# Depthwise convolution in a fused encoder kernel: 28 taps of two channel tiles go to GpSimd, 14 taps of the last tile go from TensorE to VectorE

## The reference, cut to what matters

```python
u = proj[..., Q_DIM + 2 * KV_DIM:]                    # 1024 columns
u = u[..., :CONV_CH] * jax.nn.sigmoid(u[..., CONV_CH:])     # gated: 512 channels
u = conv_general_dilated(u, conv_w[:, None, :], padding 15 on both sides,
                         feature_group_count=CONV_CH) + conv_b   # 31 taps, each channel by itself
c_out = silu(layer_norm(u, cln_g, cln_b))             # mean and variance over the 512 channels
mix = concatenate([a_out, c_out]); out = mix @ w_out
```

## Time and profile before

| | |
|---|---|
| median of 3 executions | 1344.31 us (1344.28 to 1344.64) |
| span of the profiled execution, first to last instruction | 1342.5 us |
| what lies around the span, against the median | 1.8 us |
| TensorE busy | 1335.2 us, 99% |
| VectorE busy | 1157.7 us, 86% |
| ScalarE busy | 1007.8 us, 75% |
| GpSimd busy | 44.5 us, 3% |
| the stage of the change | 16 to 104 us of the span |

### The profile page before, as it was taken

How to read it: one execution, slowest core, us unless ns; L and a number is a source line. 1 busy time by engine, 2 the same in 40 slices (tenths; PEclk the granted TensorE clock), 3 DMA queues, 4 the chain that set the end, 5 groups by cost and what they waited for, 6 DMA issues and landing times.

```text
span 1342.5 us, 19094 instructions
## 1 busy us (share of the span) xinstructions
PE 1335.2 (99%) x6779; PEld 1130.5 (84%) x6779; DVE 1157.7 (86%) x1257; ACT 1007.8 (75%) x1189; POOL 44.5 (3%) x55
## 2 busy tenths in 40 slices
PE   9999999999999999999999999999999999999998
PEld 8879999988888888888888888888888888888887
DVE  7986655557899999999999999999999999999996
ACT  7776444447878887888878788888888787888885
POOL 2000000000003000000000000000000000000100
PEclk9999999999999999999999999999999999999999
DMA  9409843476899899999999989999999999999930
GB/s 347 172 1 340 294 167 126 135 283 184 183 388 398 308 396 395 343 390 396 395 338 396 394 339 392 396 395 338 396 394 364 368 396 395 394 394 397 398 151 34
DMA packets 178661, 426.51 MB, mean 318 GB/s; under 512 B 4145, under 2 KB 14001, under 8 KB 178609
## 3 DMA queue, kind: packets, MB, share of 16 engines
q1 hardware_dynamic: 173712, 412.56, 82.1%
q0 software_dynamic: 3024, 11.01, 3.3%
q10 hardware_dynamic: 1872, 2.26, 0.5%
HBM read 419.53 MB, written 6.29 MB: 317 GB/s over the span
## 4 chain that ended last, share of the span: by engine, by line
PE 97%; DVE 2%; ACT 1%; DMA 0%; issue 0%; POOL 0%; ACTq 0%; DVEq 0%; POOLq 0%
PE G L1483 19%; PE G L1485 19%; PE G L1484 19%; PE Y L1483 11%; PE Y L1485 11%; PE Y L1484 11%; PE G L1887 2%; PE G L1677 1%; PE G L1715 1%; DVE ring L966 1%; PE Y L1685 0%; PE Y L1508 0%; DMA h<-in_x 0%; PE G L1806 0%; PE Y L1705 0%; DVE lo_ring L886 0%
## 5 line engine op out<-in xcount | busy, mean ns | idle before, releaser
L886 DVE TENSOR_TENSOR lo_ring<-ring,hi_ring 128x1024 fp32r<-128x1024 f32 x691 | 836.2, 1223 | 132.0 <-ACT hi_ring L517 92.4
L517 ACT ACTIVATE hi_ring<-ring 128x1024 fp32r<-128x1024 f32 x691 | 731.5, 1061 | 244.4 <-PE G L1485 149.8
L1483 PE MATMUL G<-hi_ring,xT_hi 128*128 128x512 f32 x896 | 353.6, 395 | 0.0
L1485 PE MATMUL G<-lo_ring,xT_hi 128*128 128x512 f32 x896 | 349.5, 390 | 0.0
L1484 PE MATMUL G<-hi_ring,xT_lo 128*128 128x512 f32 x896 | 348.8, 389 | 0.0
L1483 PE MATMUL Y<-hi_ring,mT_hi 128*128 128x512 f32 x568 | 224.1, 395 | 0.0
L1485 PE MATMUL Y<-lo_ring,mT_hi 128*128 128x512 f32 x568 | 221.4, 390 | 0.0
L1484 PE MATMUL Y<-hi_ring,mT_lo 128*128 128x512 f32 x568 | 221.2, 389 | 0.0
L1485 PEld LDWEIGHTS G<-lo_ring,xT_hi 128*128 128x128 f32 x896 | 168.2, 188 | 35.9
L1484 PEld LDWEIGHTS G<-hi_ring,xT_lo 128*128 128x128 f32 x896 | 168.3, 188 | 33.6
L1483 PEld LDWEIGHTS G<-hi_ring,xT_hi 128*128 128x128 f32 x896 | 168.3, 188 | 33.5 <-DVE lo_ring L886 0.3
(11 more groups left out here) (262 smaller groups left out, 947.8 us busy)
## 6 DMA issues: line engine op xcount, KB each, us to landing
ring<-in_moe_wg SPq DMA_DIRECT2D x56, 2048.0 KB, 12.2
ring<-in_moe_wu SPq DMA_DIRECT2D x56, 2048.0 KB, 13.2
ring<-in_moe_wd SPq DMA_DIRECT2D x56, 2048.0 KB, 13.1
ring<-in_ffn_wg SPq DMA_DIRECT2D x5, 2048.0 KB, 14.3
ring<-in_ffn_wu SPq DMA_DIRECT2D x5, 2048.0 KB, 12.9
ring<-in_ffn_wd SPq DMA_DIRECT2D x5, 2048.0 KB, 9.1
ring<-in_ple_gate_w SPq DMA_DIRECT2D x4, 2048.0 KB, 7.8
ring<-in_w_in SPq DMA_DIRECT2D x4, 1024.0 KB, 14.9
```

What stands on the lines that cost most here:

```text
L517: act.activation(hi_ring[:, n % AHEAD, :], where, ACT.Copy).then_inc(hi_done, 1)
L886: dve.tensor_tensor(lo_ring[:, n % AHEAD, :], where, hi_ring[:, n % AHEAD, :].bitcast(F32), ALU.subtract).then_inc(lo_done, 1)
L1483: pe.matmul(dst, s_hi, m_hi, start=start, stop=False, skip_group_check=True)
L1485: return pe.matmul(dst, s_hi, m_lo, start=False, stop=stop, skip_group_check=True)
```

## The change

The last 14 taps (17 to 30) of tiles 0 and 1 leave VectorE's queue. GpSimd makes them for both tiles at once, in 128x512 operations: a product into `side`, then 13 times a product into `side_part` and an addition to `side`, each waiting for the one before. VectorE adds `side` to tiles 0 and 1 behind its loop. Taps 0 to 13 of tile 3 leave TensorE (and their diagonals leave ScalarE) and become VectorE taps beside those of tile 2. TensorE keeps 17 taps of tile 3, and VectorE adds their sum from PSUM, in place of ScalarE's copy. `LATE_TAPS` has 45 entries instead of 59.

```diff
-PE_TAPS = tuple((3, k) for k in range(CONV_W))
+VECTOR_TAPS = 14
+PE_TAPS = tuple((3, k) for k in range(VECTOR_TAPS, CONV_W))
 EARLY_TAPS = tuple((c, k) for k in range(1, EARLY_ROWS) for c in range(2))
-LATE_TAPS = late_taps()
+LATE_TAPS = tuple((c, k) for k in range(CONV_W) for c in (2, 3) if c == 2 or k < VECTOR_TAPS)
+CONV_STEPS = (EARLY_ROWS + 1, EARLY_ROWS + 1, CONV_W, VECTOR_TAPS + 1)
-STEP_TAPS = (6, 6, 2, 3, 3, 2, 3, 3, 3, 0)
-assert sum(STEP_TAPS) == CONV_W
+STEP_TAPS = (4, 3, 1, 2, 1, 1, 2, 1, 2, 0)
+assert sum(STEP_TAPS) == len(PE_TAPS)
...
+    side = carve(2 * SEQ).rearrange("p (c n) -> p c n", c=2)
+    side_part = carve(2 * SEQ).rearrange("p (c n) -> p c n", c=2)
...
     (ScalarE, behind its loop)
-        act.wait_ge(conv_mm, 1)
-        act.activation(conv[:, 3, :], G[:, 3, 0:SEQ], ACT.Identity, bias=conv_b[:, 3:4]).then_inc(conv_out, 1)
...
     (VectorE, behind its loop)
+        dve.wait_ge(conv_mm, 1)
+        dve.wait_ge(conv_v[3], VECTOR_TAPS)
+        dve.tensor_tensor(conv[:, 3, :], conv[:, 3, :], G[:, 3, 0:SEQ], ALU.add).then_inc(conv_v[3], 1)
+        dve.wait_ge(side_step, 2 * (CONV_W - EARLY_ROWS) - 1)
+        for c in range(2):
+            dve.tensor_tensor(conv[:, c, :], conv[:, c, :], side[:, c, :], ALU.add).then_inc(conv_v[c], 1)
         taps(late, len(late))
         o_low(CT - 1)
         lo_upto(11 + AHEAD)
...
     (GpSimd, behind the rotary table)
+        pool.wait_ge(vec_in, 16)
+        pool.wait_ge(glu_done, 1)
+        for n, k in enumerate(range(EARLY_ROWS, CONV_W)):
+            weight = conv_w[:, 0:2, k:k + 1].broadcast_to([P, 2, SEQ])
+            if n == 0:
+                pool.tensor_tensor(side[:, :, :], upad[:, 0:2, k:k + SEQ], weight, ALU.mult).then_inc(side_step, 1)
+                continue
+            pool.wait_ge(side_step, 2 * n - 1)
+            pool.tensor_tensor(side_part[:, :, :], upad[:, 0:2, k:k + SEQ], weight, ALU.mult).then_inc(side_step, 1)
+            pool.wait_ge(side_step, 2 * n)
+            pool.tensor_tensor(side[:, :, :], side[:, :, :], side_part[:, :, :], ALU.add).then_inc(side_step, 1)
```

More of the change, by code:

```diff
@@ L345, in kernel_program @@
     qk_tr, qk_tr_copied = sem("qk_tr"), sem("qk_tr_copied")
[L346 to L349, removed]
+    sig_done, glu_done, zeros_set = sem("sig_done"), sem("glu_done"), sem("zeros_set")
+    conv_v = [sem(f"conv_v{c}") for c in range(CT)]
+    side_step = sem("side_step")
+    diag_a, conv_mm = sem("diag_a"), sem("conv_mm")
+    table_set, q_sq, k_sq = sem("table_set"), sem("q_sq"), sem("k_sq")
     sc_done, neg_done, exp_done, nrm_done = sem("sc_done"), sem("neg_done"), sem("exp_done"), sem("nrm_done")
@@ L615, in _ @@
         act.activation(qT[:, :, :], Y[:, 0:2, :].rearrange("p b (k n) -> p (b k) n", k=2), ACT.Copy).then_inc(qk_tr_copied, 1)
-        act.wait_ge(k_zero, 1)
+        act.wait_ge(zeros_set, 2)
         for u in range(2):
@@ L974, in taps @@
             del todo[:n]
-        dve.wait_ge(pads_set, 1)
+        dve.wait_ge(zeros_set, 1)
         glu(0)
@@ L1051, in _ @@
         lo_upto(11 + AHEAD)
-        for c in range(3):
-            dve.wait_ge(conv_v[c], CONV_W)
+        for c in range(CT):
+            dve.wait_ge(conv_v[c], CONV_STEPS[c])
         dve.wait_ge(mean_mm, 1)
@@ L1372, in _ @@
         pool.memset(upad[:, :, 0:PAD], 0.0)
-        pool.memset(upad[:, :, PAD + SEQ:], 0.0).then_inc(pads_set, 1)
-        pool.memset(kT[:, :, :, :], 0.0).then_inc(k_zero, 1)
+        pool.memset(upad[:, :, PAD + SEQ:], 0.0).then_inc(zeros_set, 1)
+        pool.memset(kT[:, :, :, :], 0.0).then_inc(zeros_set, 1)
         pool.wait_ge(cst_in, 16)
@@ L1723, in _ @@
         pe.wait_ge(o_lo, 3)
-        pe.wait_ge(conv_out, 1)
         pe.wait_ge(cst_in, 16)
         for n, c in enumerate((3, 0, 1, 2)):
-            if c < 3:
-                pe.wait_ge(conv_v[c], CONV_W)
+            pe.wait_ge(conv_v[c], CONV_STEPS[c])
             ins = pe.matmul(G[:, 0, 0:SEQ], mean_mat, conv[:, c, :], start=(n == 0), stop=(n == CT - 1))
```

## The result

The changed kernel takes 1366.93 us (median; 1366.60 to 1366.98) against 1344.42 us: 1.0166 times as long, 95% interval 1.0154 to 1.0178. That is 22.5 us slower; the forecast was 1365 us.

The account below looks back on a forecast made before the run. It took VectorE to lead ahead of the loop and both VectorE and TensorE to be full within it. Span 1342.5 + 21.0 - 0.4 = 1363.1, plus 1.8 around the span: 1364.9, said as 1365 us; 8-in-10 range 1351 to 1373.

Parts of the forecast that it names:

- What bounds: Ahead of the loop VectorE leads until 53.56 us; in the loop TensorE and VectorE are both full.
- The hold: From 23.7 us GpSimd's 128x512 operations hold VectorE's two-SBUF-operand work, 0.95 us each, 24 times: 21.0 us in all.
- two of the signs: Expected in the trace: GpSimd's operations 1.6 us and more beside taps; TensorE at about 0.8 in the loop.
- The relief: At the loop's end TensorE's transposes follow the last head's scaling sooner: -0.4 us.
- TensorE's clock: Around the stretched taps the granted clock may fall, slowing pieces 11 and 12: 0 to 3 us more, left out.
- The waits: Behind its loop VectorE waits for TensorE's last tap and GpSimd's last addition; both come in time, costing nothing.
- starved: Between dense taps GpSimd isn't let in, so the wait for `side_step` ends last: 1364 us, chance 0.05.
- The small hold: Beside VectorE, 0.12 us is a fixed handing-over price: 1346.8 us; chance 0.09 together with no hold.
- the half hold: GpSimd's operations hold VectorE only 0.3 to 0.65 us each: 1350 to 1357 us, chance 0.12.
- the faster case: No hold, and TensorE sets the loop, which shrinks by VectorE's 4.5 us: 1339.8 us, chance 0.05.
- two bounds: Ends of the total hold on VectorE: 9.5 us at 0.5 us held per operation, 17.1 at 0.8.

Follow-up runs that it names:

- x2: The changed kernel with GpSimd's 27 operations cut to 128x64 from 128x512, the rest of side zero: 1347.16 us.
- x4: x1 with the late taps reordered in threes (tile 2, tile 3, tile 2), so no two taps of a tile follow each other within a group: 1345.06 us.
- x1: The changed kernel without GpSimd's 27 operations; side is zeroed once, so taps 17 to 30 of tiles 0 and 1 are left out: 1346.05 us.

## Why the prediction was right, step by step

**What bounds.** Right: VectorE's queue leads from `glu(0)` to `glu(1)`, and every microsecond lost there shows. The loop is VectorE's too, in spite of TensorE's 24.00 busy of 24.00: 6 us of work taken from TensorE were worth 0.3, while 1.0 us came and went with the order of VectorE's taps alone.

**The hold.** Right in kind and close in size. The forecast was 0.95 us for each operation and 21.0 us in all, from one row in which a low part was 0.12 us longer beside 64 elements. Measured: 20.6 us, 0.76 for each of the 27. A tap with a GpSimd operation in front takes 1.31 us in place of 0.40, so 0.9 each where it is felt. One operation of VectorE between two of GpSimd, the rotary products at 50.8 (forecast 52) and `glu(1)` at 73.84 (forecast near 74) came as said. That the size came so close has some luck in it. The one row it was scaled from showed a low part; beside 64 elements a tap loses 0.05 us (x2), and eight times that would have been 0.4. And two of the signs were off: GpSimd's operations take 1.10 to 1.36 us beside taps and not 1.6 (1.9 to 2.15 only beside low parts), and TensorE is busy 21.96 of the 24 us from 74 to 98, 0.92 and not 0.8, at a granted clock of 0.93.

**The relief.** The reason given was right, the sooner transposes (0.04 us behind the scaling in place of 0.60, x4), and so was its size, 0.3 us for 0.4. But the forecast for the kernel as written had the wrong sign, since a term was missing. "VectorE's queue is unchanged up to there" did not hold: I had priced 45 late taps at the 0.40 us of a queue in which tiles take turns. In the change's order the last 17 stand alone on tile 2, about 0.1 us later each. That cost 1.0 us (x1 against x4): from `glu(1)` to the subtraction of the mean it is 0.6 us longer, not 0.4 shorter.

**TensorE's clock.** I left 0 to 3 us open. The granted clock did fall, to 0.63 in 53 to 61 us where TensorE was busy 2.23 of 8 us, and it cost nothing that shows: the chain ran through VectorE there, and the way behind `glu(1)` is 37.48 us, against 37.51 without GpSimd at a clock of 1.00.

**Not foreseen.** 0.8 us at 375 us, in front of TensorE, which come and go with the number of instructions ahead in its queue; the cause is open. The time lies 1.9 us above the forecast, and the terms account for 1.8 of it: 0.8 here, 1.0 for the relief, 0.4 at the start, less 0.4 for the hold.

**The waits and the rivals.** The wait for the side sum never bound: it was ready at 64.6 and wanted at 105. GpSimd was not starved. The small hold is ruled out by x2, the half hold by the taps' 1.31 us, the faster case by x1 and x4, where even without GpSimd's operations nothing was gained. In the sum two bounds are off by the prediction's own count (24 operations, less 1.8): a hold of 0.5 us gives 10.2 us and not 9.5, one of 0.8 gives 17.4 and not 17.1. Nothing hangs on them.

## What to carry to other kernels

GpSimd beside a full VectorE was not a third pair of hands here: a 128x512 operation made a low part or a tap with two SBUF operands 0.8 to 1.1 us longer, and a 128x2 product of 0.16 us still 0.4 to 0.8. Look for a GpSimd row whose duration jumps beside VectorE's and for the VectorE row beside it that is longer by a tenth; scaling it by the elements gives a first estimate, which for taps is too low. What freed VectorE was an operand in PSUM, and for the small product a form by a scalar, though a larger product by a scalar (128x256, SBUF to SBUF) was held; and even then the work moved has to be what sets the end.

A busy share of 100% does not say which of two full engines sets the pace: 6 us less on TensorE gave 0.3 us, and the order of VectorE's taps 1.0. Taps, sums or updates of one tile should take turns with another's.

## What the runs showed of the hardware that was not expected

A VectorE operation of 128x2 with two SBUF operands took 0.97 us beside GpSimd, six times its 0.16. A `tensor_scalar` of 128x256 with one streamed operand took 1.13 us in place of 0.41. GpSimd's 128x512 operations run at 1.04 us (product with a weight spread over the tokens) and 1.27 us (sum) when free, below and above the 1.19 us worked out. And a pause of 0.7 us on TensorE came with 28 instructions fewer some 300 us ahead of it, went when they were put back, and was absent with 36 or 40 fewer.
